# Two memory projection blocks of layer 1, run as eight quarters beside the heads of the differential attention

## The chip, the cores and the metric

The kernel runs on one core of one Trainium2 chip. The metric is device time in microseconds (us), median of several executions. The engines have names of their own here: PE is TensorE (matrix products), ACT is ScalarE, DVE is VectorE, POOL is GpSimd, and SP (SyncE) issues the loads of the weights. PSUM, where PE writes, has eight banks of 128 x 512 fp32.

## The reference, cut to what matters

Two transformer blocks run one behind the other on 256 tokens of width 1024. The first has two layers: layer 0 mixes with an mLSTM and a neighbourhood attention, layer 1 with a differential attention. In both, a cross attention to 256 memory tokens and a SwiGLU follow, with a layer norm behind each. The second block (window and global attention, convolutions, and 16 experts in each of two layers) is not touched by the change, but takes more than half of the time.

```python
for layer in range(DEPTH):                       # the first block; layer 1 is the odd one
    mix = even_mixer(...) if layer % 2 == 0 else odd_mixer(...)
    x = layer_norm(DEEPNORM_ALPHA * x + mix, ln_g[layer, 0], ln_b[layer, 0])
    xa = memory_cross_attention(x, mem, mem_wq[layer], mem_wkv[layer], mem_wo[layer])
    x = layer_norm(DEEPNORM_ALPHA * x + xa, ...)
    x = layer_norm(DEEPNORM_ALPHA * x + swiglu(x, ffn_w_gu[layer], ffn_w_down[layer]), ...)

def odd_mixer(x, w_in, lam_p, subln_g, w_out, lam_init):
    q, k, v = jnp.split(x @ w_in, 3, axis=-1)    # q and k through rope, 8 heads of 2 x 64; v 8 x 128
    ...
    s = jnp.einsum('bqhcd,bkhcd->bhcqk', qi, k) * scale       # two score maps for each head
    p = jax.nn.softmax(s, axis=-1)
    o = einsum(p[:, :, 0] - lam * p[:, :, 1], v)              # one output of 128 for each head
    o = rms_norm(o, subln_g) * (1.0 - lam_init)
    return o.reshape(B_, S, C_WIDTH) @ w_out

def memory_cross_attention(x, mem, wq, wkv, wo):
    q = (x @ wq) * (X_HEAD_DIM ** -0.5)
    k, v = jnp.split(mem @ wkv, 2, axis=-1)      # needs mem alone, not x
    ...
```

`mem @ wkv` depends on nothing that layer 1 computes. It may run anywhere before the cross attention of layer 1.

## The kernel before

**Weights.** A weight matrix is cut into blocks of 512 output columns, and a block into two units of 4 x 128 input rows (1 MB each). `weight_plan` lists the units in the order of their use, and SP loads them in this order into seven slots. A product in this block is made in three passes of rounded operands (high part of the weight by high part of the data, low by high, high by low: `passes`, L624 to L626). So each unit is split first: ACT rounds it into one of four high slots (L1734, `split_through`), then POOL subtracts in four pieces of 128 x 512 (L1639) to get the low part in place. Unit number n can be rounded when unit n - 4 has been read by PE for the last time. ACT does the splits at fixed places of its own program: `follow(block)`, which stands behind the evacuation of a block, splits the units four places further on. Each engine takes its instructions in the order of its program, and semaphores are the only link between them.

**Projections.** `project_T_halves` computes a block transposed: two banks of two column groups of 128 each, 4 chunks and 3 passes for each, so 48 products of 128 x 256 for a unit, first those of unit 0 in both banks and then those of unit 1. `kT` gets the results of memory blocks 0 and 1 (the keys), `v_rows` those of blocks 2 and 3.

**The heads of the differential attention in layer 1.** For each of 8 heads PE computes two score maps (`diff_scores`, L1014, banks 4 and 5 for an even head, 2 and 3 for an odd one), DVE takes the maxima (L2605), ACT the exponentials with their sums (`diff_exps`, L1955), DVE normalises and subtracts (`diff_normalise`, L2613 to L2619), PE transposes (`turn`, L836, bank 6), ACT evacuates (`evac_T`, L1766), and PE multiplies by the values (`value_rows`, L1023, banks 7 and 1). DVE copies the head's output (L2634), and ACT sums its squares (`o_squares`, L1966). The programs are written out by hand. PE: scores of head i + 2, turn of head i, values of head i - 1. ACT: exponentials of head i, evacuation of head i - 1, squares of head i - 3. DVE: normalise head i, maxima of head i + 2, copy of head i - 2. Scores of head i + 2 go to the banks of head i, so they wait until the exponentials of head i have read them.

**Behind the heads.** The outputs are normalised (root on ACT, L1977, product on DVE, L2644), transposed in two tiles (`turn_o`, L1033) and split into high and low parts (L1981, L2651). Then come the output projection (`odd_out`), the residual sum and layer norm on DVE (L2326 to L2350), and the transposes of x (`norm_T`, L957). The two units of memory block 0 stand on PE ahead of the two `turn_o`. Blocks 1, 2 and 3 stand behind the output projection, beside the layer norm.

The change touches `weight_plan`, the program of PE in layer 1 with its `turn_o`, and the program of ACT beside it. It adds one function on PE and one on ACT.

## Time and profile before

| | us |
|---|---|
| median of 3 executions | 2424.68 |
| lowest, highest | 2417.89, 2424.94 |
| the profiled execution | 2422.05 |
| its span (first to last instruction) | 2420.2 |

The profile is of one execution. PE is busy 91% of its span, DVE 31%, ACT 26% and POOL 31%. Its times are counted from the start of the span. A matmul's length in it holds its way through the pipeline, so lengths of neighbours overlap; the pace is read from their starts. "Idle before" is the time for which the engine had nothing, and behind the arrow stands what ended it. A row of windows gives a stretch and its length, then the busy time of PE, of its weight loads, of DVE, ACT and POOL (with their instructions), then the granted clock of PE as a share of full speed (1.00 is 2.4 GHz, 0.50 is 1.2 GHz), the DMA share and GB/s. The heads of the differential attention run from 618.5 to 659.3 us, the tail with block 0 to 672.6, the output projection to 695.1, and memory blocks 1, 2 and 3 from there to 728.

### The profile page before, as it was taken

Reading aid. Unit: us, or ns where it says so; the run is one execution under the profiler, and the core shown is the slowest. Engines: PE = TensorE matmul, PEld = TensorE weight load, DVE = VectorE, ACT = ScalarE, POOL = GpSimd, SP = SyncE. Lnnn points to the kernel's source line nnn. Section 1 sums busy time; section 2 is a strip of 40 time slices with the busy share of each in tenths; the row PEclk is TensorE's granted clock in tenths of the full one; section 3 lists DMA queues with packets and bytes.
Section 4 is the critical chain, followed back from the end, with each engine's and each line's share of the span. In section 5 each row is a group of like instructions: output and inputs, shape, how many; then the busy total and the mean of one; then the engine's idle time right before and its main releaser. Section 6 shows DMA issues by size and latency. Waiting matters only on the chain.

```text
span 2420.2 us, 32871 instructions
## 1 busy us (share of the span) xinstructions
PE 2194.9 (91%) x13382; PEld 1354.8 (56%) x13382; DVE 752.2 (31%) x1440; ACT 634.4 (26%) x925; POOL 739.4 (31%) x624
## 2 busy tenths in 40 slices
PE   7998999999799999999999999999889996888886
PEld 7876789878687898865543333333257642222221
DVE  4864220122622212377523222222147420010101
ACT  3544333434544334212512000010022420000001
POOL 7665367897283777710300000000000200000000
PEclk9999999999899999999999999999999998999997
DMA  9433759755157697441215899999962369999997
GB/s 299 140 118 126 261 199 317 244 179 178 36 182 254 208 324 241 143 177 39 86 53 209 341 427 429 429 429 428 424 232 78 134 277 423 427 428 429 429 428 307
DMA packets 151381, 635.98 MB, mean 263 GB/s; under 512 B 7816, under 2 KB 14216, under 8 KB 120920
## 3 DMA queue, kind: packets, MB, share of 16 engines
q1 hardware_dynamic: 148224, 623.78, 66.4%
q0 software_dynamic: 2608, 9.25, 1.3%
q8 instruction: 86, 1.41, 0.2%
q10 hardware_dynamic: 424, 1.22, 0.2%
q14 instruction: 39, 0.32, 0.0%
HBM read 633.17 MB, written 1.05 MB: 262 GB/s over the span
## 4 chain that ended last, share of the span: by engine, by line
PE 65%; DMA 20%; DVE 7%; ACT 3%; POOL 3%; issue 2%; SPq 1%; DVEq 0%; ACTq 0%; POOLq 0%
PE bank L1375 14%; PE bank L624 9%; PE bank L626 9%; PE bank L625 9%; DMA ring<-in_w_gate 9%; DMA ring<-in_w_up 8%; PE bank L1188 4%; PE bank L1333 3%; DMA ring<-in_w_down 3%; PE bank L847 2%; PE bank L1197 2%; PE bank L970 2%; POOL ring_r L1639 2%; PE bank L824 1%; PE bank L1205 1%
## 5 line engine op out<-in xcount | busy, mean ns | idle before, releaser
L1375 PE MATMUL bank<-ring,arena 128*32 128x512 f32 x4424 | 657.4, 630 | 120.6 <-DMA ring<-in_w_gate 53.9
L1639 POOL TENSOR_TENSOR ring_r<-ring,ring_r 128x512 fp32r<-128x512 f32 (+1 forms) x468 | 575.2, 1274 | 294.4 <-ACT ring_r L1734 265.6
L1375 PEld LDWEIGHTS bank<-ring,arena 128*32 128x32 f32 x4424 | 192.7, 115 | 560.3 <-issue 536.6
L624 PE MATMUL bank<-ring_r 128*128 128x256 f32 (+1 forms) x1504 | 463.4, 308 | 14.2 <-POOL ring_r L1639 8.6
L626 PE MATMUL bank<-xT_r,ring_r 128*128 128x256 f32 x1248 | 354.9, 284 | 0.0
L625 PE MATMUL bank<-ring_r 128*128 128x256 f32 x1104 | 312.9, 283 | 0.0
L624 PEld LDWEIGHTS bank<-ring_r 128*128 128x128 f32 x1504 | 289.8, 193 | 37.4 <-issue 18.0
L1734 ACT ACTIVATE ring_r<-ring 128x2048 fp32r<-128x2048 f32 (+1 forms) x119 | 216.7, 1827 | 289.2 <-DMA ring<-in_ffn_w_gu 141.2
L626 PEld LDWEIGHTS bank<-xT_r,ring_r 128*128 128x128 f32 x1248 | 240.1, 192 | 0.0
L625 PEld LDWEIGHTS bank<-ring_r 128*128 128x128 f32 x1104 | 211.6, 192 | 0.7 <-issue 0.5
L1668 POOL TENSOR_TENSOR arena<-const 128x1024 f32<-128x1024 f32 x6 | 12.0, 2003 | 594.8 <-DVEq L2288 525.5
L1766 ACT ACTIVATE arena<-bank 128x512 f32<-128x512 f32 (+1 forms) x144 | 83.7, 581 | 260.6 <-PE bank L836 71.9
L2256 ACT ACTIVATE arena<-bank 128x512 f32<-128x512 f32 x24 | 13.0, 594 | 489.2 <-PE bank L1375 489.2
L2969 DVE TENSOR_TENSOR x<-x,bank 128x512 f32<-128x512 f32 x80 | 52.2, 683 | 212.5 <-PE bank L1452 212.2
L1188 PE MATMUL bank<-xT,ring 128*128 128x512 f32 (+1 forms) x320 | 112.4, 509 | 3.9 <-ACTq L2204 1.9
L1639 POOL TENSOR_TENSOR spare_r<-spare,ring_r 128x512 fp32r<-128x512 f32 x76 | 100.6, 1364 | 11.9 <-ACT ring_r L1734 7.2
L1188 PEld LDWEIGHTS bank<-xT,ring 128*128 128x128 f32 x320 | 64.1, 203 | 47.8 <-issue 38.6
L2944 DVE TENSOR_TENSOR arena<-bank,arena 128x512 f32<-128x512 f32 x24 | 15.4, 685 | 234.1 <-PE bank L1375 234.1
L626 PE MATMUL bank<-ring_r 128*128 128x512 f32 x208 | 84.5, 406 | 0.0
L624 PE MATMUL bank<-ring_r,arena_r 128*128 128x512 f32 (+1 forms) x208 | 79.2, 381 | 2.2 <-POOL ring_r L1639 1.8
L1700 POOL TENSOR_TENSOR arena<-arena 128x512 f32<-128x512 f32 (+1 forms) x4 | 3.8, 952 | 246.4 <-ACTq L1772 246.2
L625 PE MATMUL bank<-ring_r,arena_r 128*128 128x512 f32 (+1 forms) x208 | 78.5, 378 | 0.0
(356 smaller groups left out, 2720.3 us busy)
## 6 DMA issues: line engine op xcount, KB each, us to landing
ring<-in_w_gate SPq DMA_DIRECT2D x52, 2048.0 KB, 17.2
ring<-in_w_up SPq DMA_DIRECT2D x52, 2048.0 KB, 17.3
ring<-in_w_down SPq DMA_DIRECT2D x40, 2048.0 KB, 18.1
ring<-in_ada_w SPq DMA_DIRECT2D x41, 1024.0 KB, 7.5
ring<-in_w_down SPq DMA_DIRECT2D x41, 1024.0 KB, 18.2
ring<-in_ffn_w_gu SPq DMA_DIRECT2D x35, 1024.0 KB, 5.6
ring<-in_w_up SPq DMA_DIRECT2D x18, 1024.0 KB, 8.7
ring<-in_w_gate SPq DMA_DIRECT2D x17, 1024.0 KB, 5.0
```

The costliest lines, as they stand in the source:

```text
L624: pe.matmul(dst, w_hi, v_hi, start=first, stop=False)
L625: pe.matmul(dst, w_lo, v_hi, start=False, stop=False)
L626: return pe.matmul(dst, w_hi, v_lo, start=False, stop=last)
L847: mm = pe.matmul(b[p0:p0 + dv, 256 * i:256 * i + 256], u["v"][kb][:, i * dv:(i + 1) * dv], probsT_of(u)[:, kb, :], start=(kb == 0), stop=( ...
L970: mm = pe.matmul(b[32 * j:32 * j + 32, :], scT[:, UK * h + k, :], ws[j][:, k], start=(h == 0 and k == 0), stop=(h == 1 and k == UK - 1))
L1188: mm = pe.matmul(b[:, 0:n], wb(c)[:, at:at + P], xT[:, c, 0:n], start=(c == 0), stop=(c == KC - 1))
L1333: mm = pe.matmul(b[:, :], src[:, t * P:t * P + P], wb(c), start=(c == 0), stop=(c == KC - 1))
L1375: mm = pe.matmul(dst[nb][CAP * b:CAP * b + CAP, :], src[:, c, CAP * b:CAP * b + CAP], rooms[b % G], start=bi_first, stop=bi_last)
L1639: pool.tensor_tensor(lo[:, c], whole[:, c], hi_of(u)[:, c, 0:n], ALU.subtract).then_inc(*signal("w_lo", (u, c)))
L1734: act.activation(hi_of(u)[:, 0:kc, 0:n_col], room_of(slot)[:, 0:kc, 0:n_col], ACT.Copy).then_inc(*signal("w_hi", u))
L1766: link(act.activation(dst, src, func))
L2969: dve.tensor_tensor(xs, xs, bank[bank_at][:, :], ALU.add).then_inc(m["sum_free"], 1)
```

## The change

Memory blocks 0 and 1 of layer 1 are computed by a new generator in quarters: one bank and one unit for each step, 24 products in place of 48. All quarters use bank 0. A bank takes two steps (unit 0, unit 1), so unit 0 is read for the last time in the third step of its block. Six of the eight steps stand in the loop over the heads (i = 1 to 6, between the scores of head i + 2 and the turn of head i), the other two ahead of the two `turn_o`. ACT evacuates bank 0 in the loop, at i = 2, 4 and 6, behind `evac_T`, and once behind the high parts of the outputs. At i = 4 and at the last one it follows with the splits of two units. The units of block 1 move ahead of those of the output projection in the loading order. The four banks of `turn_o` are fixed ones now (2 to 5).

```diff
@@ weight_plan
-            block(("mem_kv", layer, 0), w["mem_wkv"][layer], 0, UN)
+            for b in range(2):
+                block(("mem_kv", layer, b), w["mem_wkv"][layer], UN * b, UN * b + UN)
             matrix(("odd_out",), w["odd_w_out"][0])
...
-            for b in range(1, 4):
+            for b in range(2, 4):
                 block(("mem_kv", layer, b), w["mem_wkv"][layer], UN * b, UN * b + UN)
@@ PE
+            def project_T_quarters(key, src):
+                last_out[key] = key + ("out", 1)
+                parts = {}
+                for j in range(2):
+                    b = open_bank(key + ("out", j), 0)
+                    for h in range(2):
+                        if j == 0:
+                            parts[h] = split_weights(key, h)
+                        u, hi, lo = parts[h]
+                        for m in range(2):
+                            c0 = (2 * j + m) * P
+                            for c in range(UK):
+                                if j == m == 0:
+                                    chunk_split(u, c)
+                                mm = passes(b[:, SEQ * m:SEQ * m + SEQ], (hi[:, c, c0:c0 + P], lo[:, c, c0:c0 + P]), src(UK * h + c),
+                                            h == m == c == 0, h == m == 1 and c == UK - 1)
+                        if h == 1:
+                            mm.then_inc(*filled_now(key + ("out", j)))
+                            if j == 1:
+                                last_reader[unit_at[key + (1,)]] = last_fill[0]
+                        elif j == 1:
+                            half_through(key, 0, mm)
+                        yield
...
-                            b = dense_bank(("oT", g, t))
+                            b = open_bank(("oT", g, t), 2 + 2 * t + g)
...
+                    memory = itertools.chain(*(project_T_quarters(("mem_kv", layer, b), m_parts) for b in range(2)))
                     for i in range(C_HEADS + 1):
                         if i + 2 < C_HEADS:
                             diff_scores(diff_units[i + 2])
+                        if 1 <= i <= 6:
+                            next(memory)
                         if i < C_HEADS:
                             turn(diff_units[i])
                         if i:
                             value_rows(diff_units[i - 1])
-                    memory = project_T_halves(("mem_kv", layer, 0), m_parts, new_bank=side_bank)
                     for t in range(T2):
                         next(memory)
                         turn_o(t)
...
-                if layer == 1:
-                    project_T(("mem_kv", layer, 1), m_parts, new_bank=side_bank)
@@ ACT
+                    def memory_side(b, j):
+                        key = ("mem_kv", layer, b, "out", j)
+                        c = 4 * b + 2 * j
+                        act.wait_ge(*full(key))
+                        link(act.activation(kT[:, c:c + 2, :], bank_of(key)[:, :].rearrange("p (a b) -> p a b", a=2), ACT.Copy))
+                        act.sem_inc(*freed(key))
+                        if j == 1:
+                            follow(key[:-2])
                     for i in range(C_HEADS + 3):
                         if i < C_HEADS:
                             diff_exps(diff_units[i])
                         if 0 <= i - 1 < C_HEADS:
                             evac_T(diff_units[i - 1])
+                        if i in (2, 4, 6):
+                            memory_side(*divmod(i // 2 - 1, 2))
                         if i >= 3:
                             o_squares(diff_units[i - 3])
...
-                    evac_memory(layer, 0)
+                    memory_side(1, 1)
...
-                for b in range(1, 3 if layer else 1):
-                    evac_memory(layer, b)
+                if layer:
+                    evac_memory(layer, 2)
```

## Rows read from the trace of the kernel before

**Rows 1.** First line of the page: length of the profiled execution and its instruction count.

```profile
span 2420.2 us, 32871 instructions
```

**Rows 2.** Windows over four stages: stretch, length, each engine's busy time, clock, DMA.

```profile
630.10:659.30 29.20, 20.59 (x125) 17.66 (x125) 22.02 (x60) 21.48 (x79) 0.00 (x0) 0.79 0.01 2
...
659.30:672.60 13.30, 13.30 (x115) 13.30 (x115) 4.85 (x9) 3.83 (x9) 0.00 (x0) 0.99 0.23 79
...
695.10:706.40 11.30, 11.30 (x97) 11.25 (x97) 5.32 (x11) 4.69 (x5) 11.30 (x10) 1.00 0.68 243
```

**Rows 3.** Timeline of PE in the heads: start, length, line, shape, count, idle before.

```profile
632.83 1.14 PE L1014 MATMUL bank<-arena 64*128 64x256 f32 x8
...
634.30 0.66 PE L836 MATMUL bank<-const,arena 128*128 128x128 f32 x4 [0.33 <-DVE arena L2619]
634.79 1.06 PE L1023 MATMUL bank<-arena 128*128 128x128 f32 x8
...
655.09 1.11 PE L836 MATMUL bank<-const,arena 128*128 128x128 f32 x4 [1.34 <-DVE arena L2619]
656.00 3.62 PE L1023 MATMUL bank<-arena 128*128 128x128 f32 x16
```

**Rows 4.** Timeline of ScalarE, one head's turn.

```profile
637.34 0.47 ACT L1955 ACTIVATE arena<-bank,small 128x256 f32<-128x256 f32 x1
...
640.04 0.60 ACT L1766 ACTIVATE arena<-bank 128x512 f32<-128x512 f32 x1 [0.25 <-ACT arena L1955]
...
641.69 0.47 ACT L1955 ACTIVATE arena<-bank,small 128x256 f32<-128x256 f32 x1
```

**Rows 5.** Timeline of VectorE, same head.

```profile
640.93 0.18 DVE L2613 RECIPROCAL small<-small 128x4 f32<-128x4 f32 x1 [0.24 <-DVE arena L2634]
...
642.90 1.42 DVE L2605 TENSOR_REDUCE small<-bank 128x2 f32<-128x512 f32 x2
```

**Rows 6.** Timeline of PE behind the heads: second half of block 0, first to last.

```profile
665.88 0.36 PE L624 MATMUL bank<-ring_r 128*128 128x256 f32 x1
...
671.60 1.04 PE L1033 MATMUL bank<-const,arena 128*128 128x128 f32 x8
```

**Rows 7.** Timeline of VectorE: normalising the head outputs, low parts of tile 0.

```profile
662.90 2.50 DVE L2644 TENSOR_TENSOR arena<-arena,aff 128x512 f32<-128x512 f32 x4
...
667.44 0.75 DVE L2651 SCALAR_TENSOR_TENSOR x_r<-bank,lam,ring_r 128x512 fp32r<-128x512 f32 x1 [0.25 <-DVE x_r L2651]
```

**Rows 8.** Timeline of ScalarE and GpSimd: a unit's split behind the heads.

```profile
673.39 1.92 ACT L1734 ACTIVATE ring_r<-ring 128x2048 fp32r<-128x2048 f32 x1
...
675.20 1.32 ACT L1766 ACTIVATE arena<-bank 128x512 f32<-128x512 f32 x2
...
675.38 5.09 POOL L1639 TENSOR_TENSOR ring_r<-ring,ring_r 128x512 fp32r<-128x512 f32 x4 [53.27 <-ACT ring_r L1734]
```

**Rows 9.** Windows of one microsecond around the last heads: granted clock is third from last.

```profile
653.00:654.00 1.00, 0.75 (x4) 0.46 (x3) 0.90 (x4) 0.69 (x2) 0.00 (x0) 0.50 0.00 0
...
658.00:659.00 1.00, 1.00 (x7) 1.00 (x7) 0.38 (x1) 0.43 (x3) 0.00 (x0) 0.50 0.07 16
...
660.00:661.00 1.00, 1.00 (x11) 1.00 (x11) 0.08 (x1) 0.70 (x4) 0.00 (x0) 1.00 0.00 0
```

**Rows 10.** Timeline of layer 0's attention: GpSimd, and VectorE with and without it.

```profile
153.39 10.32 POOL L1639 TENSOR_TENSOR ring_r<-ring,ring_r 128x512 fp32r<-128x512 f32 x8 [14.59 <-ACT ring_r L1734]
...
159.86 1.40 DVE L2427 TENSOR_TENSOR x_r<-x,ring_r 128x256 fp32r<-128x256 f32 x1
161.70 2.16 DVE L2412 TENSOR_SCALAR arena<-arena,small 128x256 f32<-128x256 f32 x2
...
180.22 0.61 DVE L2412 TENSOR_SCALAR arena<-arena,small 128x256 f32<-128x256 f32 x2
```

**Rows 11.** Timeline in the first norm of layer 1: VectorE's last product, PE's transposes.

```profile
699.40 1.41 DVE L2350 SCALAR_TENSOR_TENSOR x<-bank,rstd,arena 128x512 f32<-128x512 f32 x2
...
722.84 1.04 PE L957 MATMUL bank<-const,x 128*128 128x128 f32 x8
```

More of the change, by code:

```diff
@@ L19 @@
+import itertools
 import math
```

## The prediction

> **What bounds the kernel now.** I read the page first for the span [rows 1], then windows over the stages that the edit touches [rows 2], and then each engine's timeline in them. The edit leaves the number of products alone: 192 for memory blocks 0 and 1 before and after. So its worth is the idle time of PE that the products fill, less the idle time that they make. Behind the heads there is none to fill: from 659.3 to 672.6 and from 695.1 to 706.4 PE is busy for the whole window [rows 2]. In the heads, from the end of head 3's scores (630.1) to the end of the last values (659.3), it is busy for 20.6 of 29.2 us at a mean clock of 0.79, so 8.6 us are idle, and some of the busy time is work at half speed. That is the whole prize.
>
> Who holds PE there? ACT needs 637.34 to 641.69, 4.35 us, for one head: 2.70 for the exponentials, 1.65 for evacuation and squares together [rows 4]. DVE takes 1.97 us to normalise (640.93 to 642.90) and another 1.4 for the maxima with small operations and the copy behind them [rows 5]. It too fills its 4.35 us. PE's own work for a head at full speed is short: two score maps 1.0 (8 products, 1.14 with the way through the pipeline), turn 0.49 (634.30 to 634.79), values 0.95 (1.06 with it) [rows 3], together 2.4. Two more engines are as full as the beat of the heads, so a quarter on PE is free only if it delays neither.
>
> **The change part by part.** All times here continue the clock of the old trace.
>
> *A quarter.* The second half of block 0 takes 665.88 to 671.60 for 48 products, 5.72 us [rows 6]. Half of it is 2.86.
>
> *Removed.* Block 1 behind the output projection: 11.3 us, all of it on the path [rows 2].
>
> *PE's work in the heads.* From 630.1 on: six quarters 17.2, turns 1 to 7 3.4, values 0 to 7 7.6, scores 4 to 7 3.9, together 32.1. The trace has PE at half speed until about 632.1 and quarter 1 starts in that, so I add 1.0: 33.1 us.
>
> *Waits that the order makes.* ACT's evacuation of a bank stands in its program ahead of the squares and of the next head's exponentials, and it waits for a quarter that PE starts only behind the scores. Queued behind this wait are the exponentials on which DVE's normalise, PE's next turn, and by the banks the scores two heads on, all depend. While ACT catches up PE has only a turn and values, 1.44 us. Evacuation costs half of the 1.65 in [rows 4], 0.8.
> - Behind quarter 2: evacuation 0.8 and the first map's exponentials 1.35 are 2.2 us, so scores 5 wait 0.75, and for the second map another 0.75: 1.5.
> - Behind quarter 4: here `follow` adds two splits. One takes ACT 1.81 from start to start (673.39 to 675.20) [rows 8], so 3.6. With evacuation 0.8, squares 0.85 and 1.35 for the first map that is 6.6, less 1.44: 5.2, and 0.8 for the second map: 6.0.
> - Behind quarter 6: evacuation 0.8, squares 0.85, both maps 2.7, normalise 2.0, less 1.44: 4.9, in front of turn 7. This includes all of a head's chain with nothing on PE beside it.
>
> Sum of waits 12.4 us. They take the place of the 8.6 us idle before, so as much idle time is made as is filled.
>
> *The clock.* In the old trace PE pauses ahead of turn 7 and the clock is 0.50 at 653 and still at 658, full again at 660 [rows 9]; turn 7 and the last values take 655.09 to 659.27, 4.2 us for 2.4 us of work [rows 3]. The new pause at that place is longer, so I keep this loss, 1.8. The pause of 5 us behind quarter 4 is new. It can cost nothing, if PE is back at full speed as it resumes, or half speed for up to as long as in [rows 9], 6.7 us, which for the scores, quarter 5 and what follows is at most 3.4. It lies nearer to the small end, because the second map's wait covers the first part: 0.5.
>
> *DVE beside POOL.* POOL is idle in the heads now [rows 2]. The two units split behind quarter 4 put eight subtractions there, 5.09 us for a unit [rows 8], from about 653.6 to 663.8, and the normalise of head 5 falls in it. Layer 0 shows what that does: a pair of SBUF scalings takes 2.16 us beside POOL and 0.61 without, and a product of two SBUF operands 1.40 [rows 10]. The normalise of head 5 has such a pair and two such products. Ends: 0, if all fits behind quarter 5, and 4.1, if each takes what layer 0 shows and the next turn waits for all of it. Quarter 5 covers about 2 us of the wait and part of the rest ends in ACT's own queue: 0.8.
>
> The Trainium skill, SBUF — State Buffer, section Who interferes with whom, says why: a VectorE instruction in a two-port mode and GpSimd lock each other out of a shared pair of ports for a whole instruction, and two SBUF operands contend with GpSimd's reads. It speaks against this edit, and the trace agrees (2.16 us against 0.61).
>
> So the heads take 33.1 + 12.4 + 1.8 + 0.5 + 0.8 = 48.6 us from 630.1, to 678.7. Before they ended at 659.3: 19.4 later.
>
> *The tail.* Before, 13.3 us from the last values to the end of the second `turn_o` [rows 2]. The first normalised output was there 4.3 us behind the last values: DVE's first of four products starts at 662.90 and takes about 0.65 [rows 7], hidden by 5.7 us of block 0. Quarter 7 covers 2.86 of that, so PE waits 1.5; then 0.8, quarter 8 2.86, 0.9: 9.0 us, 4.3 less. The low parts of tile 0 were ready at 668.2 [rows 7], 3.1 behind the start of `turn_o` at 665.09; the new order asks for them 4.5 behind it. That stays hidden.
>
> *Cover of the layer norm.* Without block 1, PE comes to the transposes of x 11.3 us sooner than at 722.84, at about 711.5 on the same clock. DVE's last product of the norm ends at 700.8 [rows 11]. 10.7 us are left, so this costs nothing; if DVE were late by more, each microsecond would be on the path.
>
> *The other moves, together 0.* The order of loads shifts by two units, with all seven slots filled before the heads as now. The split of the first two units of the projection moves from ahead of the heads into them. The last evacuation has the place of the old one. Bank 0 is asked for again only in the projection's second block, 11 us later. If a load or split were late here, the nearest price is one unit's split, 1.9 + 1.3 us.
>
> **The sum.** 19.4 - 4.3 - 11.3 = +3.8 us. The profiled execution took 2422.05, so 2425.9. The runs shown reach from 2417.89 to 2424.94 and their median is 2424.68, which with 3.8 gives 2428.5. The profiled one is a little below their median. Between the two I take 2427.
>
> **The rivals.**
> - *The beat of the heads gives way to PE's work.* If ACT evacuates without being late, because there is more slack than I see, PE is the bound: 33.1 us from 630.1 on, tail as above. 33.1 - 29.2 - 4.3 - 11.3 = -11.7: 2413 from the median, 2410 from the profiled execution. For it: ACT has 7.7 us of idle time in the stretch [rows 2]. Against it: the waits above follow from the order of the programs, and ACT's idle time lies in small pieces.
> - *Only the splits are cheap.* The two splits could fall where ACT has to wait anyway. Then the second wait shrinks by 3.6 and DVE is not disturbed: 3.8 - 3.6 - 0.8 = -0.6: 2423. That is still no change.
> - *The clock (slower).* Two pauses of 5 us come 15 us apart, with a beat of starts and stops between them. If the second low stretch joins the first, quarter 5, quarter 6 and the turn, values between them (8.6 us of work) run at 1.2 GHz: +8.6 in place of the 0.5. 3.8 + 8.1 = +11.9: 2436. It decides as soon as the clock is still 0.50 when quarter 6 begins. For it: the mean clock of 0.79 in a stretch with shorter pauses [rows 2]. Against it: quarters are dense, and in the dense work behind the heads the clock came back by 660 [rows 9]. The Trainium skill, TensorE: Matmul & The Clock Gate, section HAM oscillation, has the rule that idle gaps between bursts bring the clock down each time; that is this case.
>
> **How the numbers follow.** 0.3% of the median, 7.3 us, is about what a measurement can tell from no change. Forecast: 0.55, good to about 5 us, since each of six waits may be off by one. Splits cheap: 0.14. PE-bound or most of the way to it: 0.14. Clock: 0.17. Faster takes the third and a little of the forecast's lower end: 0.15. Slower takes the clock and 0.05 of the forecast's upper end: 0.21. The rest, 0.64, is no change. The range reaches to 2414 (near the PE-bound case) and 2438 (clock).
>
> **What would show it.** Three pauses of PE in the new heads: about 1.5 us ahead of and in scores 5, 5 to 6 ahead of scores 7 behind two splits on ACT, and 5 ahead of turn 7. Last values near 678 to 679. A wait of about 1.5 us ahead of the first `turn_o`, and none ahead of the output projection. Some scalings and products of head 5 on DVE over 1 us. PE without a pause from there to the memory attention. The prediction is wrong if the heads end before 670 (PE's work then sets the beat), or if windows show 0.50 through quarters 5 and 6.

## The result, and the profile after

The changed kernel took 2432.30 us in the median of 7 executions (2424.80 to 2432.75), the kernel before 2420.18 in 7 (2417.89 to 2424.94). The ratio is 1.0038, with an interval of 1.0024 to 1.0052: slower by 9.2 us (5.8 to 12.6). A second comparison of the same two, in the experiments below, gave 1.0023 (1.0002 to 1.0044), 5.6 us. The medians alone lie further apart, by 12.1 and 8.7 us; all differences below go by the ratios. The forecast was 2427, +3.8. The first result lies a little past the 0.3% that I had set as the bound of no change, the second a little inside it; the direction is that of the sum, the size is larger. The profiled execution took 2424.80 us, 2.75 more than the profiled one of before.

First line of the page of the kernel after, then windows over the first two stages of [rows 2]: the heads behind the scores of head 3, and the tail (stretch, length, busy time of PE, its loads, DVE, ACT and POOL with counts, clock, DMA share, GB/s).

```profile
span 2423.0 us, 32871 instructions
...
628.30:678.70 50.40, 39.53 (x272) 36.13 (x271) 25.92 (x60) 26.92 (x85) 9.96 (x8) 0.87 0.13 43
678.70:687.70 9.00, 8.15 (x65) 7.76 (x65) 4.76 (x9) 3.92 (x9) 0.00 (x0) 0.96 0.35 117
```

PE is idle for 10.9 of 50.4 us in the heads, where it was for 8.6 of 29.2 [rows 2]. The change put 17 us of products into the heads and there is more idle time than before: on balance the products filled none of it. The tail is 9.0 us, as worked out.

Timeline of PE in the kernel after: start, length, line, shape, count, and idle time before. L1041 are the scores, L863 the turns, L1050 the values, L626 to L628 the quarters, L1060 is `turn_o`, L984 the transposes of x for the projections behind the norm, L997 the first product with `ada` weights.

```profile
616.87 2.99 PE L1041 MATMUL bank<-arena 64*128 64x256 f32 x16 [2.24 <-DVEq L2326]
...
638.79 1.13 PE L1041 MATMUL bank<-arena 64*128 64x256 f32 x4 [0.68 <-ACTq L1985]
640.07 1.13 PE L1041 MATMUL bank<-arena 64*128 64x256 f32 x4 [0.15 <-ACTq L1985]
...
645.49 1.14 PE L1041 MATMUL bank<-arena 64*128 64x256 f32 x8
...
649.48 0.60 PE L863 MATMUL bank<-const,arena 128*128 128x128 f32 x4
649.91 1.06 PE L1050 MATMUL bank<-arena 128*128 128x128 f32 x8
656.12 3.35 PE L1041 MATMUL bank<-arena 64*128 64x256 f32 x8 [5.15 <-ACTq L1985]
659.40 0.58 PE L626 MATMUL bank<-ring_r 128*128 128x256 f32 x1
...
663.62 0.60 PE L863 MATMUL bank<-const,arena 128*128 128x128 f32 x4
...
674.15 1.12 PE L863 MATMUL bank<-const,arena 128*128 128x128 f32 x4 [4.89 <-DVE arena L2657]
...
682.71 1.26 PE L1060 MATMUL bank<-const,arena 128*128 128x128 f32 x8 [0.85 <-DVE arena L2682]
...
726.67 1.04 PE L984 MATMUL bank<-const,x 128*128 128x128 f32 x8
...
757.02 0.63 PE L997 MATMUL bank<-ring,const 128*32 128x512 f32 x3
```

The three pauses are there, in their places and sizes: 0.68 and a small one in scores 5, 5.15 ahead of scores 7, 4.89 ahead of turn 7. What the sum did not have right is the row behind the second pause: eight score products take 3.28 us from start to start (656.12 to 659.40), where scores 6 took 1.07 (645.49 to 646.56, the start of quarter 4).

Two things are in these 3.28 us. One is the order of the two score maps. When both banks are free, the products of the two maps start 13 ns apart, pair by pair, and the eight take 1.07 us together. In scores 5 the second map was released 1.28 us behind the first, and its four products took 1.06 us alone (640.07 to 641.13, the start of quarter 3). So a late second map costs 1.27 us at full clock, and not the 0.75 or 0.8 that I had counted. The other is the clock, which is 0.50 here: 0.9 us.

Timeline of ACT in the kernel after, ahead of that pause: the evacuation of a quarter's bank (L2001) waited 4.32 us for quarter 4, and two splits (L1761), the squares of a head (L1993) and only then the exponentials (L1982) follow.

```profile
649.68 0.60 ACT L2001 ACTIVATE arena<-bank 128x512 f32<-128x512 f32 x1 [4.32 <-PE bank L628]
650.45 1.91 ACT L1761 ACTIVATE ring_r<-ring 128x2048 fp32r<-128x2048 f32 x1 [0.18 <-ACT arena L2001]
652.27 1.89 ACT L1761 ACTIVATE ring_r<-spare 128x2048 fp32r<-128x2048 f32 x1
...
654.86 0.47 ACT L1982 ACTIVATE arena<-bank,small 128x256 f32<-128x256 f32 x1
```

Timeline of DVE in the kernel after, its normalise of head 5 (first fence), and of POOL, the two groups of subtractions beside it (second fence):

```profile
657.45 0.18 DVE L2651 RECIPROCAL small<-small 128x4 f32<-128x4 f32 x1 [8.61 <-ACTq L1799]
657.67 0.95 DVE L2652 TENSOR_SCALAR small<-small,lam 128x2 f32<-128x2 f32 x1
658.65 2.60 DVE L2654 TENSOR_SCALAR arena<-arena,small 128x256 f32<-128x256 f32 x2
661.29 1.78 DVE L2657 SCALAR_TENSOR_TENSOR arena<-arena,small 128x256 f32<-128x256 f32 x2
```

```profile
652.44 4.93 POOL L1666 TENSOR_TENSOR ring_r<-ring,ring_r 128x512 fp32r<-128x512 f32 x4 [31.94 <-ACT ring_r L1761]
657.33 5.06 POOL L1666 TENSOR_TENSOR spare_r<-spare,ring_r 128x512 fp32r<-128x512 f32 x4
```

The normalise ends 5.5 us after it began (657.45 to about 662.99, where DVE's next group starts), against 1.97 in [rows 5]. PE doesn't wait for it here: turn 5 starts at 663.62 without idle time.

Windows over the stretch behind the second pause; the granted clock is third from last.

```profile
656.00:658.00 2.00, 1.88 (x6) 1.60 (x7) 0.51 (x2) 1.60 (x6) 2.00 (x3) 0.50 0.00 0
...
660.00:662.00 2.00, 2.00 (x11) 2.00 (x11) 1.97 (x2) 1.44 (x6) 2.00 (x2) 0.50 0.00 0
662.00:664.00 2.00, 2.00 (x18) 2.00 (x18) 1.97 (x4) 0.00 (x0) 0.39 (x1) 0.92 0.00 0
```

**A measure for the stage.** Executions of either kernel differ by more than the effect, so in traces I compare a stretch: from the first scores to the first `ada` product. Everything that the edit moves lies in it. Timeline of the kernel before, its two ends:

```profile
618.48 3.76 PE L1014 MATMUL bank<-arena 64*128 64x256 f32 x16 [2.23 <-DVEq L2288]
...
753.17 0.63 PE L970 MATMUL bank<-ring,const 128*32 128x512 f32 x3
```

It is 134.7 us before and 140.2 after, +5.5. The parts: heads behind scores 3 +21.2 (50.4 for 29.2), tail -4.3, block 1 -11.3 (the transposes of x come 39.0 us behind the tail's end, before 50.2), up to the end of scores 3 -0.2. Each stage is read from one execution, and there is one trace of the kernel before. The runs below show that the clock alone moves the stage of one program by 2 us and more, so differences of that size between two stages are not an effect of an edit unless the rows show where they lie. One such place comes back below: quarter 1 took 2.93 us in the kernel after, and between 2.93 and 4.27 in the others, by the clock that it starts at.

### The profile page after: what moved, and what is told of

Read it like the earlier page. It is cut to its first block, busy times and chain, and to the rows that moved or that the text cites. A ratio compares the mean times of both kernels' runs of the same rounds, so it can differ in the third digit from the quotient of the medians.

```text
span 2423.0 us, 32871 instructions
## 1 busy us (share of the span) xinstructions
PE 2191.5 (90%) x13382; PEld 1355.8 (56%) x13382; DVE 757.1 (31%) x1440; ACT 634.0 (26%) x925; POOL 739.4 (31%) x624
## 4 chain that ended last, share of the span: by engine, by line
PE 65%; DMA 19%; DVE 6%; POOL 4%; ACT 3%; issue 2%; SPq 1%; DVEq 0%; ACTq 0%; POOLq 0%
PE bank L1402 14%; PE bank L626 9%; PE bank L628 9%; PE bank L627 9%; DMA ring<-in_w_gate 9%; DMA ring<-in_w_up 8%; PE bank L1215 4%; PE bank L1360 3%; DMA ring<-in_w_down 3%; POOL ring_r L1666 2%; PE bank L874 2%; PE bank L997 2%; PE bank L1224 2%; PE bank L851 1%; PE bank L1232 1%
## 5 line engine op out<-in xcount | busy, mean ns | idle before, releaser
L626 PE MATMUL bank<-ring_r 128*128 128x256 f32 (+1 forms) x1504 | 465.2, 309 | 13.7 <-POOL ring_r L1666 8.0
L628 PE MATMUL bank<-xT_r,ring_r 128*128 128x256 f32 x1248 | 354.9, 284 | 0.0
L626 PEld LDWEIGHTS bank<-ring_r 128*128 128x128 f32 x1504 | 289.9, 193 | 39.1 <-issue 19.9
L1761 ACT ACTIVATE ring_r<-ring 128x2048 fp32r<-128x2048 f32 (+1 forms) x119 | 216.6, 1827 | 286.6 <-DMA ring<-in_ffn_w_gu 138.8
L628 PEld LDWEIGHTS bank<-xT_r,ring_r 128*128 128x128 f32 x1248 | 240.0, 192 | 0.0
L628 PE MATMUL bank<-ring_r 128*128 128x512 f32 x208 | 84.7, 407 | 0.0
L626 PE MATMUL bank<-ring_r,arena_r 128*128 128x512 f32 (+1 forms) x208 | 79.4, 382 | 2.2 <-POOL ring_r L1666 1.8
```

The lines of the kernel that those rows point to most:

```text
L626: pe.matmul(dst, w_hi, v_hi, start=first, stop=False)
L628: return pe.matmul(dst, w_hi, v_lo, start=False, stop=last)
L1761: act.activation(hi_of(u)[:, 0:kc, 0:n_col], room_of(slot)[:, 0:kc, 0:n_col], ACT.Copy).then_inc(*signal("w_hi", u))
```

## The experiments

Theory: ACT takes its program in order, so an evacuation that waits for a quarter, and two splits behind it, hold up the exponentials on which the rest of the heads depends; and PE resumes from each pause at half speed. Rivals: DVE held by POOL makes the loss; or the loss is elsewhere and the pauses cost little. "Stage" below is the stretch just defined, of the one profiled execution. The comparisons of e1 to e4 are of 12 executions with 35 of the kernel before, those of e5, e6 and e8 of 12 with 29. "In us" is the ratio's difference from 1 times the median of the kernel before. e7 and e9 are one execution each.

| kernel | stage | ratio to before | in us |
|---|---|---|---|
| before | 134.7 | | |
| after | 140.2 | 1.0038 (1.0024 to 1.0052) | +9.2 |
| after again (e6) | 142.1 | 1.0023 (1.0002 to 1.0044) | +5.6 |
| splits later (e1) | 136.3 | 1.0035 (1.0009 to 1.0060) | +8.5 |
| evacuation later (e2) | 131.2 | 0.9979 (0.9958 to 1.0000) | -5.1 |
| both later (e3) | 126.1 | 0.9973 (0.9957 to 0.9988) | -6.5 |
| pauses filled (e4) | 138.1 | 1.0014 (0.9994 to 1.0034) | +3.4 |
| POOL held (e5) | 143.8 | 1.0055 (1.0032 to 1.0078) | +13.3 |
| splits later, one execution (e7) | 140.3 | | |
| both later, POOL held (e8) | 127.8 | 0.9977 (0.9955 to 0.9998) | -5.6 |
| filled, POOL held, one execution (e9) | 139.7 | | |

**e1, the two splits later.** Queued behind the root of the head norms in place of behind quarter 4's evacuation:

```
-                        if j == 1:
+                        if (b, j) == (1, 1):
                             follow(key[:-2])
 ...
                     act.activation(o_std, o_var, ACT.Sqrt).then_inc(*signal("rstd", "diff"))
+                    follow(("mem_kv", layer, 0))
```

> The changed kernel, but the two splits that stood behind quarter 4 on ScalarE now stand behind the root of the head outputs. Theory (order of ScalarE's queue): PE's pause of 5.15 us ahead of scores 7 falls to about 1.5, the clock is not 0.50 at 656 to 662, head 5's normalise takes 2.0 us and not 5.5; the heads end 5 to 6 us sooner. The splits come late for the output projection, whose first two units POOL then feeds at 1.27 us a piece: 1 to 2 us of waits come back there. 4 us faster than the changed kernel, level with the kernel before to +3. Rival (clock): the pause goes, but the turn 7 pause still brings the clock down, 2 us or less gained. Rival (the loss is outside the heads): less than 2 us.

Measured: 2430.58 us median (2412.99 to 2445.36) against 2423.83. Timeline of PE in e1, from turn 4 to turn 5:

```profile
651.31 0.60 PE L863 MATMUL bank<-const,arena 128*128 128x128 f32 x4
...
654.30 1.13 PE L1041 MATMUL bank<-arena 64*128 64x256 f32 x4 [1.49 <-ACTq L1985]
...
659.56 0.60 PE L863 MATMUL bank<-const,arena 128*128 128x128 f32 x4
```

The pause shrinks from 5.15 to 1.49, by 3.66, just the 3.6 that I had counted for two splits. From turn 4 to turn 5 it takes 8.25 us in place of 14.14: 3.66 less by the pause and 2.2 by the clock, which stays full (0.9 in scores 7, which take 2.33 with the late second map here too, and 1.3 in quarter 5). The pause ahead of turn 7 stays at 4.89, as it must. In the stage 3.8 us are gone, since later parts give some back (the first `turn_o` waits 1.15 instead of 0.85, and the projection takes 1.9 us more, as the splits and POOL's subtractions now come late for it). The times of whole executions don't show it: the interval of e1 covers both the kernel after and nearly no change, and it spreads over 32 us. This comparison is inconclusive; the trace is not.

**e7, the same kernel in another execution.**

> The kernel with the two splits behind the root once more, one look at a trace, since its executions reached from 2413 to 2445. Theory: in a long execution the products that normalise the head outputs, which have two SBUF operands and start as GpSimd starts ten us of subtractions, are held until GpSimd is through (up to 10 us in place of 1). Rival: the heads and this place look as in the trace there is, and the time is lost in layer 0.

Measured: 2431.55 us, stage 140.3, 4 longer than in e1, with the same pause. The theory fell: the last of the four products that normalise the head outputs took 1.79 us in e1 and in e7, and the other three 0.7 each. The rival was right that this place looks alike, but the heads do not. Windows of e1 behind it (first fence), then e7: its row of scores 7 in the timeline of PE, and a window behind that (second and third fence).

```profile
655.00:657.00 2.00, 1.85 (x9) 1.06 (x9) 1.26 (x5) 1.56 (x6) 0.00 (x0) 1.00 0.46 177
657.00:659.00 2.00, 2.00 (x20) 2.00 (x19) 1.93 (x4) 1.73 (x8) 0.00 (x0) 1.00 0.00 0
```

```profile
657.65 3.35 PE L1041 MATMUL bank<-arena 64*128 64x256 f32 x8 [1.49 <-ACTq L1985]
```

```profile
661.00:663.00 2.00, 2.00 (x10) 2.00 (x10) 1.79 (x4) 1.82 (x8) 0.00 (x0) 0.50 0.00 0
```

The same program with the same pause of 1.49 us runs at full clock in one execution and at 0.50 in the other; turn 4 to turn 5 takes 8.25 and 11.23, and quarter 1 is 1 us longer too (3.97 against 3.00). So the pauses have two prices: one that the order of the programs sets, the same in each execution, and the clock behind them, which varies by up to 3 us with the execution. It is one reason for the spread of the times.

**e2, the evacuations one head later.** The bank is then full when ACT comes to it.

```
-                        if i in (2, 4, 6):
+                        if i in (3, 5, 7):
```

> The changed kernel, but ScalarE evacuates bank 0 one head later (i = 3, 5, 7 in place of 2, 4, 6), so the exponentials of the next head no longer stand behind the wait for the quarter; the two splits stay behind the second evacuation. Theory (order of the queue): the pauses of 0.8 us in scores 5 and 5.15 us ahead of scores 7 go, that ahead of turn 7 falls from 4.9 to about 3, one of 1.6 comes ahead of turn 6. Heads end some 9 us sooner; 9 us faster than the changed kernel, 4 faster than the one before. Rival (clock): as fast only if the windows show 1.00 through the heads; 3 us gained otherwise. Rival (outside the heads): less than 2 us.

Measured: 2417.19 us (2408.17 to 2432.55), faster than before by up to 0.4% or equal to it. No pause stands ahead of scores 4 to 7. One of 5.26 is left, ahead of turn 6, behind the splits; I had expected it in two parts, 1.6 there and about 3 ahead of turn 7, where now there is none. Timeline of ACT (first fence) and of PE (second fence) in e2:

```profile
649.62 0.60 ACT L1793 ACTIVATE arena<-bank 128x512 f32<-128x512 f32 x1 [1.38 <-PE bank L863]
650.40 0.60 ACT L2001 ACTIVATE arena<-bank 128x512 f32<-128x512 f32 x1 [0.18 <-ACT arena L1793]
```

```profile
663.91 1.12 PE L863 MATMUL bank<-const,arena 128*128 128x128 f32 x4 [5.26 <-DVE arena L2657]
```

The evacuation waits 0.18 in place of 4.32. The wait ahead of it, for the head's turn, is 1.38: ACT waits for the things that the heads need, and no longer for a quarter. The stage is 9.0 us shorter than in the kernel after, although quarter 1 ran at the low clock (4.09 us against 2.93). This is the largest single part of the loss.

**e3, both.**

> Both edits: evacuation one head later and the two splits behind the root. Theory: no pause over 1.5 us is left in the heads and PE's own work sets the beat, 5.3 us for a head with a quarter; heads end 11 to 12 us sooner than in the changed kernel, 1 to 2 us come back as waits for POOL in the output projection. 10 us faster than the changed kernel, 5 to 8 faster than the one before (2413). Rival (clock): 5 us faster than the changed kernel. Rival (outside the heads): less than 3 us.

Measured: 2416.55 us (2410.49 to 2426.76), 0.27% faster than before with an interval of 0.12 to 0.43%, and faster than the kernel after. Timeline of PE in e3, the turns of heads 3 and 4 (one beat), the last turn and the first `turn_o`:

```profile
655.79 0.60 PE L863 MATMUL bank<-const,arena 128*128 128x128 f32 x4
661.21 0.60 PE L863 MATMUL bank<-const,arena 128*128 128x128 f32 x4
...
673.58 0.66 PE L863 MATMUL bank<-const,arena 128*128 128x128 f32 x4 [1.30 <-DVE arena L2658]
...
680.41 1.26 PE L1060 MATMUL bank<-const,arena 128*128 128x128 f32 x8 [1.33 <-DVE arena L2683]
```

A head takes 5.42 us, which is PE's own work: quarter 2.92, turn 0.43, values 0.99, scores 1.07. So ACT and DVE, both full for a beat of 4.35 [rows 4, 5], are no longer what holds the heads. The forecast's first rival, PE as the bound, comes true with the same quarters when ACT's program asks for each bank a head later. The stage is 14.1 us shorter than after and 8.6 shorter than before. The rival gave -11.7; 1.3 are left ahead of turn 7 and 0.9 in the projection, where three products wait for POOL's splits, which come late now.

**e4, the pauses kept, but PE busy in them.** Five products of 128x512 whose results are not used, ahead of scores 7 and of turn 7:

```
+                    def fill_pause(n):
+                        pe.wait_ge(bank_free[7], filled[7])
+                        for _ in range(n):
+                            pe.matmul(bank[7][:, :], con("ones"), con("winmask"), start=True, stop=True)
 ...
+                        if i in (5, 7):
+                            fill_pause(5)
```

> The changed kernel with ten extra products of 128 x 512 fp32 whose result is not used, five ahead of scores 7 and five ahead of turn 7, so that PE is busy through both pauses; nothing else moves. Theory (order of the queue): the pauses stay as long, only their low clock goes: scores 7, quarter 5, turn 7, values 6 and 7 and the start of quarter 7 at full speed. 2 to 4 us faster than the changed kernel. Rival (clock): the low clock is the greater part of the loss, and in some executions lasts through quarter 6; 6 to 9 us faster, level with the kernel before, and the spread of the times (2425 to 2433) goes. Rival (outside the heads): no difference, spread as before.

A window over the heads of e4 (first fence), and PE's rows for scores 7 and turn 5 (second fence):

```profile
628.00:678.00 50.00, 46.14 (x306) 37.26 (x307) 26.39 (x62) 28.11 (x89) 10.01 (x8) 1.00 0.13 43
```

```profile
655.77 1.13 PE L1041 MATMUL bank<-arena 64*128 64x256 f32 x4 [0.86 <-ACTq L1993]
...
662.83 0.66 PE L863 MATMUL bank<-const,arena 128*128 128x128 f32 x4 [1.63 <-DVE arena L2665]
```

Measured: 2425.06 us (2421.92 to 2435.13). The clock is 1.00 over the whole 50 us. The splits' price is untouched: from values 4 to scores 7 it takes 6.21 us, as in the kernel after. The stage is 2.1 us shorter; the interval of the times overlaps that of the kernel after (e6), so they alone don't show a gain. Without one new wait it would be 3.7: with quarter 5 at full speed PE waits 1.63 us ahead of turn 5, for the normalise of head 5 beside POOL. The low clock had covered it.

**e5, POOL held until the head outputs are normalised.**

```
+                if u == unit_at[("odd_out", 0, 0)]:
+                    pool.wait_ge(*after("oT", ("o_norm", 1, T2 - 1)))
```

> The changed kernel, but GpSimd begins the subtractions of the output projection's first two units only when all four products that normalise the head outputs are done, so that it works beside no VectorE instruction of the heads. Theory (contention): head 5's normalise takes 2.0 us in place of 5.5 and no execution can see it held longer; the pauses of PE stay (5.15, 4.9). The heads end at most 1 us sooner in a profiled execution, and 1 to 2 us come back ahead of the projection, so the median is the changed kernel's or 2 us less. If the executions at 2432 of the changed kernel are ones in which VectorE was held longer in the heads, the spread narrows to its lower group, about 6 above the kernel before. Rival (the spread comes from elsewhere in the program): spread as in the changed kernel.

Measured: 2433.82 us (2428.01 to 2446.31) against 2421.35. The normalise of head 5 is back at 2.0 us, yet turn 4 to turn 5 takes 14.91 us (14.14 and, in e6, 14.85 without the hold): nothing gained, because PE is held by its own low clock meanwhile. The projection pays 2.3 us, waiting for the splits that POOL now does late, and quarter 1 took 4.23 us at the low clock, 1.3 more than in the kernel after. The spread of the times did not narrow either (2428 to 2446). So the normalise is slower beside POOL, but that is not what made this change slower.

**e6, the changed kernel again**, measured together with e5, e7 and e8.

> The changed kernel once more, on this chip, beside the variants. Theory: from the start of the scores to the first product of the modulation weights 140 us as in the profile there is (134.7 before), 5.5 of difference, and the median 5 to 9 above the kernel before. If the profiled execution is a long one, its trace shows where: VectorE held by GpSimd in layer 0 or in the heads of layer 1, or the clock. Rival: 5.5 us is all there is and the rest of the 9 measured was chance, then the median is 5 above.

Measured: 2430.08 us (2422.11 to 2434.00) against 2421.35. Pauses 5.15 and 4.88, the same to 0.01 us. The stage is 2.0 us longer than in the first execution of the same program: quarter 1 with the turn ahead of it 1.26 longer, turn 4 to turn 5 0.71 longer, both by a clock that stays low longer. This window row of e6 has 0.50, where the kernel after had 0.92:

```profile
662.00:664.00 2.00, 2.00 (x11) 2.00 (x11) 1.96 (x3) 0.82 (x4) 1.65 (x2) 0.50 0.00 0
```

**e8, both later and POOL held.**

> Evacuation one head later, the two splits behind the root, and GpSimd held until the four normalising products are done. Theory: as the variant with both edits (126 us from the scores to the modulation weights, 8.6 less than before), with the products at 0.69 us and not 0.96, no long executions from this place, and 1 us more of waits for GpSimd in the projection. 7 to 8 us faster than the kernel before, with a narrower spread than without the hold. Rival: the hold costs more than it gives, 3 to 5 us faster than before.

Measured: 2416.61 us (2408.14 to 2425.32), the same as e3 as far as this comparison can tell. I had expected a narrower spread, and it is not: 17 us here, 16 in e3. The stage is 1.7 longer, of which 1.3 is quarter 1 at the low clock (4.27 us against 2.93) and 0.3 the projection. With the splits behind the heads there is nothing on POOL to keep from DVE.

**e9, pauses filled and POOL held.** This tells whether the low clock and the contention lie side by side.

> The changed kernel with both edits together: five more products of 128x512 (fp32, const, bank 7, results unused) ahead of scores 7 and ahead of turn 7, and GpSimd's first unit of the projection held until the head outputs are normalised. With the pauses filled alone the clock was full throughout, but a wait of 1.63 us stood ahead of turn 5, for VectorE's normalise of head 5, which took 5.5 us beside GpSimd's subtractions; from turn 4 to turn 5 it took 13.71 us, and 14.14 in the changed kernel, where the low clock made quarter 5 slower and no wait was seen. Theory (two costs side by side: whichever is taken away, the other holds PE): with both gone the wait ahead of turn 5 disappears and turn 4 to turn 5 takes 13.71 - 1.63 = 12.1 us; the last values end 1.6 us nearer to the first scores than with the pauses filled alone. Rival (the wait ahead of turn 5 comes of ScalarE's late exponentials, not of GpSimd): it stays at 1.3 to 1.7 and turn 4 to turn 5 stays at 13.7. Both: the stage from first scores to the first ada product about 138 to 139, since holding GpSimd costs about 2 us in the projection.

Timeline of PE in e9, scores 7 and the pause ahead of turn 7; between them PE is idle only for 0.15 us, ahead of the second map of scores 7:

```profile
673.64 1.13 PE L1041 MATMUL bank<-arena 64*128 64x256 f32 x4 [0.86 <-ACTq L1995]
...
689.45 0.66 PE L863 MATMUL bank<-const,arena 128*128 128x128 f32 x4 [0.60 <-DVE arena L2667]
```

The wait ahead of turn 5 is gone, and turn 4 to turn 5 takes 11.90 us, where either remedy alone gives 13.7 (e4) or 14.9 (e5). The two costs run side by side and only the longer shows. The stage, 139.7, is no shorter than in e4: the hold costs its 2 us in the projection, and this execution began its quarter 1 at half speed (1.2 us). The whole execution took 2437.90 us, the longest of the profiled ones; its first scores began 12 to 17 us later than in all but e3 and e8, and the last section shows a part of that.

## Why the prediction was right, and where its size was not

Each term in the order of the prediction, with what the profiled execution of the kernel after shows, from the end of scores 3 at 628.28 to the start of quarter 7 at 678.34 (50.1 us; predicted 48.6). Each is a difference of starts, less that of the same work at full speed elsewhere in the timeline (turn 0.43, values 0.99, scores 1.07, quarter 2.92):

| term | predicted | measured |
|---|---|---|
| PE's work at full speed | 32.1 | 32.7 |
| quarter 1 at half speed | 1.0 | 0 here, 1.3 in e6 |
| waits of scores 5 | 1.5 | 2.0 (0.75 ahead of them, 1.27 by the second map) |
| pause ahead of scores 7 | 5.2 | 5.2 |
| scores 7 and quarter 5 over their work | 0.8 wait + 0.5 clock | 3.5 (1.3 second map, 2.2 clock) |
| wait ahead of turn 7 | 4.9 | 4.95 |
| turn 7 and last values at low clock | 1.8 | 1.8 |
| DVE beside POOL | 0.8 | 0 |

- **Work and waits.** Right, and this is the mechanism: ACT's evacuation waits for PE's quarter, the exponentials stand behind it, and the idle time that the quarters fill comes back elsewhere. e2 and e3 show it by taking it away: -9.0 and -14.1 us.
- **The late second map.** The sum took it that PE would work on the first map's products (half of 1.0 us) while the second was late, and counted 0.75 and 0.8. But the four products of one map alone take as long (1.06) as the eight of both maps together (1.07), so the late map cost 1.27 each time, 1.0 us more in all.
- **The clock behind quarter 4.** This is the term that was mis-sized most. I had put 0.5 on it, near the small end of 0 to 3.4, arguing that the second map's wait covers the first part. It cost 2.2: e1, with the same late second map at full clock, takes 0.9 less in scores 7 and 1.3 less in quarter 5. With the 0.7 more of e6 it reaches 2.9. The argument looked at one wait and not at the whole stretch. [rows 9] had shown half speed for at least 5 us in a stretch where no pause of PE was longer than the 2.80 ahead of turn 6 (shown below; the clock was 0.50 already at 653, before the pause of 1.34 began). What PE does at that speed, scores 7 and 12 or more of quarter 5's 24 products, nothing else covered. The rival with +8.6 did not come: the clock is back before quarter 6 (0.92 at 662, 1.00 from 664). By the rule of the Trainium skill, TensorE: Matmul & The Clock Gate, section HAM oscillation, idle gaps between bursts bring the clock down; here the trace agrees in both of the long pauses, and e4 and e9, which fill them, run at 1.00 behind them. e7 against e1 shows that it is not a fixed price. The row of the kernel before, turn 6:

```profile
651.74 0.66 PE L836 MATMUL bank<-const,arena 128*128 128x128 f32 x4 [2.80 <-DVE arena L2619]
```

- **DVE beside POOL.** The mechanism was right and stronger than I had made it (5.5 us instead of 2.0), but its effect was nil in this kernel, since the low clock covered it. By e4 and e9 it is 1.6 to 1.8 us, as soon as the clock no longer covers it. The two terms were not to be added; the larger should have been taken.
- **The tail, block 1, the norm's cover.** -4.3 of -4.3, -11.3 of -11.3, and no new wait in the layer norm. The first `turn_o` waited 0.85 instead of 1.5, since low clock again made quarter 7 longer.
- **The sum.** +5.5 in the stage against +3.8, and +7.4 in e6; the two comparisons gave +9.2 (5.8 to 12.6) and +5.6 (0.5 to 10.7). The stage of e6 lies in both intervals, that of the first execution 0.3 us below the first. That execution was the fastest of its seven, and e6 shows that the clock can cost 2 us more; I can't divide the rest further. Some of the agreement is luck. In the heads the sum was short by 1.5 us, which is 3.3 that it had too low (work 0.6, second maps 1.0, clock 1.7) less 1.8 that did not come (quarter 1 at half speed, DVE beside POOL). And the time itself (2427 against 2432.30) started from a median of 2424.68 in three executions; with seven it is 2420.18, from which the same sum gives 2424.0.

The chance of "slower" was 0.21, and I reserved it for the long low clock. By the first comparison this is what came, by the second the change stays inside the bound of 0.3%. The excess over the sum is a smaller amount of the same thing, with the second maps beside it. The rival "only the splits are cheap" fell: e1 shows that they cost their 3.66 us. "PE is the bound" fell for this kernel, and is what e3 reaches.

What stays open: why the rest of the program, which is the same in all, takes 2281 to 2298 us in the profiled executions (their time less the stage). e3 and e9 have one part of it, below. And the clock at the start of the heads, which moves quarter 1 by up to 1.3 us, was not tried.

## What to carry to other kernels

Before putting work into an engine's idle time, walk through the program of every other engine that has to serve that work: an evacuation queued directly behind the producer that it waits for holds everything behind it, and one position later in the program turned a loss of 0.2 to 0.4% into a gain of 0.2% (e2; its interval reaches to 0), and of 0.27% with the splits moved too (e3). Long, uncritical operations such as splits belong behind the last operation on which the chain depends. Where two groups of products run as pairs, as the two score maps do here, a late second group costs its whole time and not half of it. Where a new pause comes before work on PE, count that work at half speed up to what the nearest rows show, and take overlapping delays (low clock here, a held DVE there) as the larger of them, not as their sum.

## What the runs showed of the hardware that I had not expected

A VectorE operation can be held for far longer than one GpSimd instruction. In e3's profiled execution, in layer 0, far ahead of the edit, VectorE's operation on 128x4 elements (first fence: e3; second: POOL beside it) stood for 19.57 us and ended as GpSimd's row of 24 subtractions did (92.46 to about 122.15). PE was idle from 110.03 to 124.20, 12 us of it during this hold. The same operation in the kernel before, beside the same subtractions, took 1.10 (third fence).

```profile
102.60 19.57 DVE L2573 SCALAR_TENSOR_TENSOR small<-small 128x4 f32<-128x4 f32 x1 [0.15 <-DVE arena L2567]
```

```profile
92.46 15.00 POOL L1666 TENSOR_TENSOR ring_r<-ring,ring_r 128x512 fp32r<-128x512 f32 x12 [7.93 <-DVE arena L2536]
107.39 5.00 POOL L1666 TENSOR_TENSOR spare_r<-spare,ring_r 128x512 fp32r<-128x512 f32 x4
112.34 9.81 POOL L1666 TENSOR_TENSOR ring_r<-ring,ring_r 128x512 fp32r<-128x512 f32 x8
```

```profile
103.56 1.10 DVE L2534 SCALAR_TENSOR_TENSOR small<-small 128x4 f32<-128x4 f32 x1 [0.15 <-DVE arena L2528]
```

In that execution it was GpSimd's second group that took longer, 9.61 us for four subtractions instead of 5.00. One of the four took 5.46, beside a VectorE product of two SBUF operands of 128x4096 that took 5.49:

```profile
108.41 9.61 POOL L1639 TENSOR_TENSOR spare_r<-spare,ring_r 128x512 fp32r<-128x512 f32 x4
```

The Trainium skill, SBUF — State Buffer, section Who interferes with whom, has the one that issues first hold the shared ports for its whole instruction; the trace shows an operation of VectorE held over about 16 of GpSimd's, 1.25 us each, in one execution and for about one in another. Of the eleven profiled executions e3 and e9 have this hold (19.57 us in both), and they are the two whose first scores came last (630.58 and 633.06 us, 616.38 to 625.70 in the others). In all eleven, one operation of the convolutions at the start of layer 0 was held for 15.3 to 16.6 us. In the kernel before:

```profile
39.40 16.48 DVE L2495 TENSOR_SCALAR arena<-arena,cols 128x256 f32<-128x256 f32 x1 [0.32 <-DVE xT_r L2363]
```

Beside it GpSimd issued four transfers and then did 11 subtractions. What starts such a hold, and how much of the spread of the times it makes, was not tried.

That the granted clock behind one and the same pause differs between executions (e1 and e7, the kernel after and e6) was new to me too: 1.00 or 0.50 behind 1.49 us of idle time, and 3 us of time with it. So was the way in which the products of two score maps, on 64 rows each, run as pairs: eight in 1.07 us together, and four in 1.06 when the other map is late.
